# One attention front on one core: the keys' weight tile first, latent products between the keys' two halves, one activation table load less, squares summed over halves before the matrix product

## The reference, cut to what matters

```python
h = x @ w_in
c_q, k, v, k_idx, w_idx = jnp.split(h, [256, 384, 512, 640], axis=-1)   # 256 latent columns first
c_q = rms_norm(c_q, g_cq)                  # needs the mean of c_q's squares
q = (c_q @ w_uq).reshape(B, T, 16, 64)
q_idx = (c_q @ w_iq).reshape(B, T, 8, 128)
k_idx = layer_norm(k_idx, g_ik, b_ik)
...                                        # rotary turns of q, k, q_idx, k_idx
rel = jax.nn.relu(jnp.einsum('bqhd,bsd->bhqs', qib, k_idx))
score = jnp.einsum('bqh,bhqs->bqs', wb, rel)     # causal mask, then the 64 best keys of each query
...                                        # softmax attention over the selected keys, @ w_o
```

## Time and profile before

| what | value |
|---|---|
| median of 3 runs | 1050.39 us (1050.32 to 1051.92) |
| the profiled execution's own time | 1050.05 us |
| its span in the trace | 1048.2 us |
| PE busy | 1028.5 us, 98% of the span |
| POOL busy | 794.5 us, 76% |
| ACT busy | 560.6 us, 53% |
| DVE busy | 464.2 us, 44% |

### The profile page before, as it was taken

The page is one execution under the profiler, slowest core; times in us unless marked ns, Lnnn a source line. Parts: engine busy times, 40 slices in busy tenths (PEclk is TensorE's granted clock), DMA queues, the critical chain, the costliest instruction groups (busy, mean ns, idle before and its releaser), DMA issues.

```text
span 1048.2 us, 17970 instructions
## 1 busy us (share of the span) xinstructions
PE 1028.5 (98%) x7744; PEld 951.0 (91%) x7744; DVE 464.2 (44%) x757; ACT 560.6 (53%) x779; POOL 794.5 (76%) x238
## 2 busy tenths in 40 slices
PE   7989999999999999999999999999999999999997
PEld 7868899998889997899998899999999988999986
DVE  4874263349825775317321142921253252533303
ACT  6684544443358775454444256466568356444420
POOL 4826898879678756889888779687674968988880
PEclk9999999999999999999999999999999999999999
DMA  9405555555545332765555356454443655555541
GB/s 361 155 2 182 219 201 188 188 191 198 198 169 196 123 121 85 250 249 195 184 189 195 134 194 235 164 198 144 178 162 116 207 197 187 197 202 189 184 151 40
DMA packets 27454, 186.59 MB, mean 178 GB/s; under 512 B 3168, under 2 KB 3424, under 8 KB 5872
## 3 DMA queue, kind: packets, MB, share of 16 engines
q1 hardware_dynamic: 25184, 178.83, 47.2%
q10 hardware_dynamic: 2192, 6.62, 2.0%
HBM read 184.39 MB, written 1.05 MB: 177 GB/s over the span
## 4 chain that ended last, share of the span: by engine, by line
PE 93%; ACT 2%; DVE 2%; POOL 1%; DMA 1%; issue 0%; DVEq 0%; SPq 0%; POOLq 0%
PE ps L409 29%; PE ps L411 29%; PE ps L410 28%; ACT arena L874 1%; PE ps L1528 1%; PE ps L1199 1%; DMA stage<-in_tiles 1%; PE ps L2242 1%; ACT arena L883 0%; POOL wl L393 0%; PE ps L760 0%; DVE arena L1087 0%; PE ps L2247 0%; PE ps L1546 0%; DVE arena L1082 0%
## 5 line engine op out<-in xcount | busy, mean ns | idle before, releaser
L393 POOL TENSOR_TENSOR wl<-stage,wh 128x2048 fp32r<-128x2048 f32 x165 | 762.6, 4644 | 209.3 <-ACT wh L389 189.0
L389 ACT ACTIVATE wh<-stage 128x2048 fp32r<-128x2048 f32 (+1 forms) x167 | 317.8, 1907 | 113.5 <-DMA stage<-in_tiles 112.7
L409 PE MATMUL ps<-xh,wh 128*128 128x256 f32 x1328 | 369.7, 278 | 1.4 <-DVE wl L536 1.4
L410 PE MATMUL ps<-xl,wh 128*128 128x256 f32 x1328 | 368.0, 277 | 0.0
L411 PE MATMUL ps<-xh,wl 128*128 128x256 f32 x1328 | 368.0, 277 | 0.0
L409 PEld LDWEIGHTS ps<-xh,wh 128*128 128x128 f32 x1328 | 249.7, 188 | 3.8 <-DVE wl L536 1.6
L410 PEld LDWEIGHTS ps<-xl,wh 128*128 128x128 f32 x1328 | 250.1, 188 | 0.1
L411 PEld LDWEIGHTS ps<-xh,wl 128*128 128x128 f32 x1328 | 249.3, 188 | 0.0
L409 PE MATMUL ps<-wh,xh 128*128 128x512 f32 (+2 forms) x400 | 134.4, 336 | 1.2 <-DVE xl L1136 0.9
L411 PE MATMUL ps<-wh,xl 128*128 128x512 f32 (+2 forms) x400 | 132.4, 331 | 0.0
L410 PE MATMUL ps<-wl,xh 128*128 128x512 f32 (+2 forms) x400 | 132.3, 331 | 0.0
(11 more groups left out here) (381 smaller groups left out, 1136.6 us busy)
## 6 DMA issues: line engine op xcount, KB each, us to landing
stage<-in_tiles SPq DMA_DIRECT2D x167, 1024.0 KB, 4.9
arena<-in_ln_g ACTq DMA_DIRECT2D x4, 512.0 KB, 3.8
arena<-in_ln_b ACTq DMA_DIRECT2D x4, 512.0 KB, 5.1
arena<-in_x_t SPq DMA_DIRECT2D x1, 1024.0 KB, 5.4
x_res<-in_x SPq DMA_DIRECT2D x1, 1024.0 KB, 21.0
out<-x_res SPq DMA_DIRECT2D x4, 256.0 KB, 2.0
stage<-in_tiles SPq DMA_DIRECT2D x1, 544.0 KB, 9.1
arena<-in_pre_mix_norm ACTq DMA_DIRECT2D x1, 512.0 KB, 6.8
```

Of the source, the lines that this page charges most:

```text
L389: nc.scalar.activation(tile_of(wh, n, *part), tile_of(stage, n, *part), ACT.Copy).then_inc(hi_done, 1)
L393: nc.gpsimd.tensor_tensor(tile_of(wl, n), tile_of(stage, n), tile_of(wh, n).bitcast(F32), ALU.subtract).then_inc(lo_done, 1)
L409: mm(out_, lh, rh, start=start, stop=False, skip_group_check=skip)
L410: mm(out_, lh, rl, start=False, stop=False, skip_group_check=skip)
```

## The change

What it does, part by part:

1. SP loads tile 1 before tile 0. ACT makes tile 1's high part in two halves (`KEY_HALVES`, 544 columns each) before tile 0's quarters, and DVE the low parts in the same order.
2. PE makes the index keys of token half 0 first, then the latent products, then the index keys of half 1. One warm-up product less.
3. The first activation table loaded is the one with the sine. The high part of tile 3 moves ahead of L939; the sine and the second table load move ahead of the squares.
4. DVE adds the squares of the two latent halves, `cqt[:, 0]` and `cqt[:, 1]`, in SBUF (signal `sq_sum`), so that PE needs 2 products for the column sums, not 4. They now stand in the middle of `query(2, 1)`, between its two halves of columns.
5. Tile 5's high and low parts are each made in two halves: the first high half on ACT behind `index_turned(1)`, the second behind `index_turned(0)`; the first low half on POOL ahead of `dsa_pool`, the second behind it.

```diff
-        his = [1]
+        def lo_half(n, h):
+            c = (h * TW // 2, (h + 1) * TW // 2)
+            return nc.gpsimd.tensor_tensor(tile_of(wl, n, *c), tile_of(stage, n, *c), tile_of(wh, n, *c).bitcast(F32), ALU.subtract)
+
+        his = [2]
...
         def setup_dve(dve):
             for c in range(4):
                 x_lo(dve, c, x_raw)
+            for c in range(2):
+                dve.wait_ge(first_hi.sem, c + 1)
+                first_low(1, KEY_HALVES[c])
...
-            dve.wait_ge(hi_done, 2)
-            first_low(1, (0, KD * IW))
...
         def setup_x_act(act):
-            nc.scalar.preload_act_table_set("natural_log_exp_and_others")
+            nc.scalar.preload_act_table_set("trig_and_small")
...
+            act.wait_ge(stage_in[1], 16)
+            for part in KEY_HALVES:
+                nc.scalar.activation(tile_of(wh, 1, *part), tile_of(stage, 1, *part), ACT.Copy
+                ).then_inc(first_hi.sem, first_hi.up())
...
-            keep_warm(7, 12)
+            keep_warm(7, 11)
+            index_keys(0)
             for c in range(4):
-                pe.wait_ge(first_lo.sem, c + 1)
-                pe.wait_ge(x_ready.sem, x_ready.due(pe))
+                pe.wait_ge(first_lo.sem, c + 3)
...
-            low_ready(pe, 1)
-            for t in range(2):
...
+            index_keys(1).then_inc(used, 1)
+
+            def squares_summed():
+                pe.wait_ge(sq_sum.sem, sq_sum.due(pe))
+                for t in range(2):
+                    last = mm(ps[:, 3, t:t + 1], cqt[:, 0, t * P:(t + 1) * P], mean_hd[:, 0:1], start=True, stop=True)
+                last.then_inc(ss_ps.sem, ss_ps.up())
...
-            pe.wait_ge(sq_done.sem, sq_done.due(pe))
-            for t in range(2):
-                for k in range(2):
-                    last = mm(ps[:, 3, t:t + 1], cqt[:, k, t * P:(t + 1) * P], mean_hd[:, 0:1], start=k == 0, stop=k == 1)
-            last.then_inc(ss_ps.sem, ss_ps.up())
-            query(2, 1, (6, 7)).then_inc(iq_ps.sem, iq_ps.up())
+            query(2, 1, (6, 7), between=squares_summed).then_inc(iq_ps.sem, iq_ps.up())
...
-            hi_until(act, 3)
             late_loads(act)
+            setup_act2(act)
+            nc.scalar.preload_act_table_set("natural_log_exp_and_others")
             act.wait_ge(cq_ready.sem, cq_ready.due(act))
             for k in range(2):
                 last = nc.scalar.activation(cqt[:, k, :], ps[:, CQ_BANK[k], 0:T], ACT.Square)
             last.then_inc(sq_done.sem, sq_done.up())
-            setup_act2(act)
-            nc.scalar.preload_act_table_set("natural_log_exp_and_others")
...
-            hi_until(act, 5)
+            hi_until(act, 4)
...
             index_turned(1)
+            hi_half(5, 0)
...
             index_turned(0)
+            hi_half(5, 1)
...
             V.tensor_scalar(wi, bank2(1)[:, :, ID:IW], float(IH ** -0.5 * ID ** -0.5), None, ALU.mult)
+            dve.wait_ge(sq_done.sem, sq_done.due(dve))
+            V.tensor_tensor(cqt[:, 0, :], cqt[:, 0, :], cqt[:, 1, :], ALU.add).then_inc(sq_sum.sem, sq_sum.up())
...
-            for n in range(RING):
+            for n in (1, 0, *range(2, RING)):
                 load(sp, n)
...
-            hi_until(act, 2)
+            hi_until(act, 3)
...
-            for n in range(2, 6):
+            for n in range(2, 5):
                 lo(pool, n)
+            pool.wait_ge(first_hi.sem, 6)
+            lo_half(5, 0)
             dsa_pool(pool)
+            pool.wait_ge(hi_done, 6)
+            lo_half(5, 1).then_inc(lo_done, 1)
```

More of the change, by code:

```diff
@@ L328, in build @@
         numbers, trig_done, reduced_t, trig_t_done = signals("numbers trig_done reduced_t trig_t_done")
-        first_hi, first_lo, wo_lo = signals("first_hi first_lo wo_lo")
+        first_hi, first_lo, wo_lo, sq_sum = signals("first_hi first_lo wo_lo sq_sum")
         QUARTER = TW // 4
+        KEY_HALVES = ((0, KD // 2 * IW), (KD // 2 * IW, KD * IW))
         cqh_done, sq_done, ss_ps, rs_cq, iq_ps, iq_done, q_ps, kr_done, kis_ready, k_rot = signals(
@@ L415, in low_ready @@
             if n == 1:
-                pe.wait_ge(first_lo.sem, 5)
+                pe.wait_ge(first_lo.sem, 2)
             elif n == LAST_WO:
@@ L541, in setup_dve @@
                 x_lo(dve, c, x_raw)
+            for c in range(2):
+                dve.wait_ge(first_hi.sem, c + 1)
+                first_low(1, KEY_HALVES[c])
             for c in range(4):
                 if c < 3:
-                    dve.wait_ge(first_hi.sem, c + 1)
+                    dve.wait_ge(first_hi.sem, c + 3)
                 else:
-                    dve.wait_ge(hi_done, 1)
+                    dve.wait_ge(hi_done, 2)
                 first_low(0, (c * QUARTER, (c + 1) * QUARTER))
-            dve.wait_ge(hi_done, 2)
-            first_low(1, (0, KD * IW))
             dve.wait_ge(pos_in, 16)
@@ L634, in setup_x_act @@
                 else:
-                    ins.then_inc(hi_done, 1)
+                    ins.then_inc(hi_done, 2)
         def x_lo(dve, c, src):
@@ L693, in dsa_pe, with index_keys @@
             pe.wait_ge(consts.sem, consts.due(pe, 2))
-            keep_warm(7, 12)
+            keep_warm(7, 11)
+            def index_keys(t):
+                x = slice(t * P, (t + 1) * P)
+                for k in range(KD):
+                    if t == 0 and k % 4 == 0:
+                        pe.wait_ge(first_lo.sem, k // 4 + 1)
+                    if t == 0 and k % 2 == 0:
+                        pe.wait_ge(x_ready.sem, x_ready.due(pe))
+                    o = k * IW
+                    last = mm3(ps[:, 1, t * T:t * T + IW], (xh[:, k, x], xl[:, k, x]),
+                               (tile_of(wh, 1, o, o + IW), tile_of(wl, 1, o, o + IW)), k == 0, k == KD - 1)
+                return last
+            index_keys(0)
             for c in range(4):
-                pe.wait_ge(first_lo.sem, c + 1)
-                pe.wait_ge(x_ready.sem, x_ready.due(pe))
+                pe.wait_ge(first_lo.sem, c + 3)
                 for m in range(2):
@@ L703, in dsa_pe, with query @@
             last.then_inc(used, 1)
-            low_ready(pe, 1)
-            for t in range(2):
[L706 to L713, removed]
+            index_keys(1).then_inc(used, 1)
[4 more added lines that the diff above has]
+                last.then_inc(ss_ps.sem, ss_ps.up())
+            def query(n, t, bank, first=None, between=None):
                 low_ready(pe, n)
@@ L722, in query @@
                         last.then_inc(first.sem, first.up())
+                    if between and c == 0:
+                        between()
                 return last
@@ L960, in dsa_act, with hi_half @@
             act.wait_ge(rs_cq.sem, rs_cq.now())
-            hi_until(act, 5)
+            hi_until(act, 4)
+            def hi_half(n, h):
+                act.wait_ge(stage_in[ring(n)], come[n])
+                part = (h * TW // 2, (h + 1) * TW // 2)
+                ins = nc.scalar.activation(tile_of(wh, n, *part), tile_of(stage, n, *part), ACT.Copy)
+                if h:
+                    ins.then_inc(hi_done, 1)
+                    his[0] += 1
+                else:
+                    ins.then_inc(first_hi.sem, first_hi.up())
             def index_plain(t):
```

## The result

Five runs of the changed kernel gave 1055.63 us median (1054.33 to 1055.98), five of the kernel before beside them 1050.37 (1050.16 to 1051.92); the ratio is 1.0038, with a 95% interval of 1.0027 to 1.0048. That is slower by more than the 0.2% that can be told from no change. The ratio on 1050.39 gives 1054.4, inside the range of 1051.0 to 1055.0; the median of these runs itself lies 0.6 above that range (the quotient of the two medians would be 1.0050). The profiled execution took 1054.51 with a span of 1052.7, 4.5 above the span before.

What follows compares the result with a forecast made beforehand. PE was taken to bound the kernel, with DVE and ACT setting the pace in the front and softmax. 1.48 + 1.88 = 3.36 on 1050.05 gives 1053.4; with 0.34 for the median, 1053.7, range 1051.0 to 1055.0.

Steps and rivals of the forecast that it cites:

- Start of PE: Front: with the keys' tile first, PE starts at 10.05 for 10.54, 0.48 earlier; cover for the latent tile 0.7 us.
- Latents and ACT's order: Front: latents end 2.2 later, `hh` at 18.56 for 16.36; ACT's squares end at 21.56.
- The addition: Front, DVE: the sum of the squares, issued near 22.0, waits for POOL's subtraction and ends at 24.64.
- +1.48: Front: `index_rope(1)` begins at 26.97 for 25.49 because PE waits for the held addition of the squares.
- the halved sums: Front, PE: 4 of 8 column-sum records are gone from behind the wait, 0.43.
- Tile 5 in halves: Softmax: POOL's second low half (2.30) delays tile 6, whose subtraction holds DVE's first group of `normalised` products (L916).
- +1.88: Softmax: ACT's copy L883 of pair 0 begins at 59.63 for 57.75, with the first part's shift taken off.
- ACT runs back to back from there, so nothing gives the time back: Softmax, after the copy of pair 0: ACT has no gaps, so the delay stays to the end.
- more is lost: Front: PE's clock falls after 2.3 us idle, 4.1 more (1057.8), or the latent tile is late (near 1055); together 0.06.
- the rivals with one hold: Only the front's addition is held: 1051.9, chance 0.10; only the softmax's L916 is held: 1051.5, chance 0.09.

Runs made afterwards that it cites:

- a_again: The changed kernel profiled and timed once more, unaltered; ratio 1.0040 against the kernel before.
- a_fill_both: The changed kernel with unused products on PE in two waits, 8 before the column sums and 7 before the softmax's first transposes; ratio 1.0026.
- a_nosum: The changed kernel without DVE's addition of the squares, PE making four column-sum products as before; ratio 1.0024.
- a_psum: The changed kernel with the second square row written to PSUM, so the addition has one input in SBUF; ratio 1.0012.
- a_warm14: The changed kernel with 14 warm-up products on PE in place of 11; ratio 1.0042.
- a_order: The changed kernel with the first two tiles in the old order, tile 0 and the latent products first; ratio 1.0035.
- b_five: The kernel before with tile 5's halves on ACT and POOL and nothing else; ratio 1.0031.
- a_fill: The changed kernel with 16 unused products on PE before the softmax's first transposes only; ratio 1.0047.
- a_tile6: The changed kernel with tile 6's low part on POOL moved behind the wait for the last softmax pair; ratio 1.0021.
- d_psum_tile6_warm: The changed kernel with the second square row in PSUM, tile 6's low part behind the last softmax pair, and 14 warm-up products; ratio 0.9987.

## Why the prediction was right, and where it was low

- **Start of PE** 10.05: measured 10.03, 9.98 and 9.91 (changed kernel, a_again, a_fill_both). Right, and with its cover: PE waited for no latent quarter.
- **Latents and ACT's order**: `hh` forecast for 18.56, 18.47 in a_again; 20.27 in the first profile, because of the clock. Right, but for a fall that I had not placed there.
- **The addition**: forecast end 24.64, 0.28 behind POOL. Measured 24.47 in a_again (POOL's end 24.19) and 24.66 in a_fill_both (24.38): 0.28 in both. The term +1.48 came out at 1.34 and 1.52. a_nosum and a_psum show the cause. Inside it the halved sums were priced at 0.43 and are worth 0.36.
- **Tile 5 in halves**: the low half 2.35 for the 2.30 taken, tile 6's end at 59.37 for the forecast 59.3, the first product of a_fill_both's group 2.58 long (56.87 to 59.45, its POOL ending at 59.37). The term +1.88 came out at 1.84 to 1.90 in seven kernels (a_again, a_warm14, a_order, a_nosum, a_psum, b_five, a_fill_both); in the changed kernel's first profile it was 2.40, with the clock already low during the transposes.
- **"ACT runs back to back from there, so nothing gives the time back"**: that step was incomplete. Nothing gives it back, but more is lost: where PE stood idle for 1.9 behind the group and its clock then fell, the way from the first copy to the last grew by 0.81 to 1.05 (a_again, b_five, a_psum, a_warm14); in a_nosum, a_order and a_fill_both, with a full clock there, it did not grow.
- **The rival "more is lost"** had the right mechanism and too small a chance (0.06, together with others), the wrong place first of all, and the wrong price. I put it behind the addition's wait, where it came in three of five profiles with that wait unfilled, and charged 4.1 for 18 products; there it cost at most 1.3 (`index_rope(1)` at 28.36 in a_fill for 27.01 in a_fill_both; 28.15 in a_warm14, 27.56 in a_order), since `index_rope(1)` waits for only six products behind the column sums and the clock was full again at 28.5. In the softmax, where I did not look for it, it came in five of seven with the wait unfilled.

So the mechanism and both terms of the sum were right: 3.36 forecast, 3.2 (span) to 3.3 (last copy) measured in the one profile with both holds and a full clock. The missing term, 0.7 or more for the clock, makes a_again's 3.97 of them (its median: 1054.72 against 1050.54). That the result still lies in the range is owed to the width of the range, which was drawn for the rivals with one hold; the sum itself was low by 0.7 (1054.4 for 1053.7), and by 1.9 if one goes by the median of the changed kernel's runs.

The rest is not explained. The changed kernel's first runs lie another 0.9 above a_again's, with granted clocks of 0.994 to 0.998, and more falls would fit; only one of them has rows. But the clock can't be all of it: two of a_again's executions at 0.999 took 1054.97 and 1055.46, longer than the profiled one at 0.998 (1053.70).

One place where such a loss stands in rows at full clock is known. In a_tile6 DVE's work is 1.2 behind the kernel before at 619 us, 2.2 behind at a copy that begins at 640.25 for 638.04, 3.5 behind at one that begins at 700.83 for 697.36, and 2.7 behind at the end of the span; a_nosum goes the same way, from 0.5 over 2.8 to 2.0. So 1.5 was lost for good in the front of the recurrence. The changed kernel's first profile lost 0.4 there and a_again nothing. The cause was not tested.

## What to carry to other kernels

Before an instruction with two inputs in SBUF, or a fast TENSOR_SCALAR, is put on DVE, look at what POOL does at that moment: a 0.4 us addition on the critical path cost what was left of POOL's 9 us stretch. One operand in PSUM undid the hold of the addition at no cost, and with it the four small matrix records saved were worth their 0.36 us, although the new dependence passes through two other engines; POOL's work moved out of the softmax undid the hold of the group for 0.2 at most, but it held another instruction of DVE, one that nothing waits for so closely. A wait that leaves PE idle for some 2 us should be priced as the wait plus, in many executions, about 1 us of half clock behind it. Where such a wait cannot be removed, a few products without a use in it are worth a trial: in the three waits filled here (one of a_fill, two of a_fill_both) the clock stayed full, though it had also stayed full in 2 of 5 and 2 of 7 unfilled ones. And read more than one execution: the first profile of this kernel showed the forecast time for the wrong reason.

## What the hardware showed that I had not expected

- The granted clock fell to 0.50 in single stretches within a span whose mean was 0.996 to 0.998. Each fall came after a stretch in which PE had stood idle (0.7 to 2.6 us) or run short products, and in some executions of one and the same kernel but not in others: the changed kernel had one at 12.6 in its first profile and none there in its second.
- A late stage can hide a hold: at half clock the latents were late enough for the addition to miss POOL's stretch, and `index_rope(1)` came within 0.2 of where the hold had put it.
- The issue of the same small DMA on ACT's queue took 0.45 in most executions and 0.72, 0.77 and 1.19 in others (a_warm14, d_psum_tile6_warm, the changed kernel), and ACT's next work waited for it.
- One table load between the sine and the squares cost 1.28 and nothing behind it (22.22 + 1.28 = 23.50, next instruction at 23.51).
